# First stage of an RWKV and attention kernel: tile by tile, with two buffers for the mixes

## The reference, cut to what matters

```python
mod_x = jax.nn.silu(c) @ mod_w[i] + mod_b[i]        # and mod_c from c_ctx
sh_x, sc_x, g_x = jnp.split(mod_x[:, None, :], 3, axis=-1)
h_x = rmsnorm(x, norm_g[i]) * (1.0 + sc_x) + sh_x   # and h_c
prev = jnp.pad(h[:, :-1], ((0, 0), (1, 0), (0, 0)))
nxt = jnp.pad(h[:, 1:], ((0, 0), (0, 1), (0, 0)))
xx = 0.5 * (prev + nxt) - h
lerp = lambda j: h + xx * mu[j]
r, k, v, gate = (lerp(j) @ w_in[j] for j in range(4))   # 1024 x 1024 each
lerp(4) @ w1, lerp(5) @ a1                               # 128 columns each (two directions)
...
x = x + g_x * d_x                                    # d_x is the mixer's output
```

## Time and profile before

| | us |
|---|---|
| median of 3 runs | 4448.01 |
| lowest and highest | 4444.34 and 4450.34 |
| the profiled execution | 4446.85 |
| its span in the trace | 4445.1 |
| busy in it: PE, PEld, DVE, ACT, POOL | 3809.0, 2148.3, 1544.3, 1354.1, 206.0 |
| first stage, first product to last | 87.86 to 490.99 |
| mean granted clock of PE | 0.939 |

### The profile page before, as it was taken

One profiled execution on the slowest core, in us unless ns is written; L12 is line 12 of the kernel. 1 busy time (PEld: TensorE's weight loads), 2 busy tenths in 40 slices (PEclk: granted clock), 3 DMA queues, 4 the chain that ended last, 5 costly groups with the idle time before them and its releaser, 6 DMA issues. The chain is left out here.

```text
span 4445.1 us, 76078 instructions
## 1 busy us (share of the span) xinstructions
PE 3809.0 (86%) x32246; PEld 2148.3 (48%) x32246; DVE 1544.3 (35%) x3747; ACT 1354.1 (30%) x2940; POOL 206.0 (5%) x199
## 2 busy tenths in 40 slices
PE   5999577777787699999898888999959988699997
PEld 2555366666666444666466543333335455233332
DVE  2000366666676112443236531111122174211112
ACT  2000234444433122332446422222224263222221
POOL 0000000000000000010010000000012000000000
PEclk7999789989999899999999989999979999899998
DMA  5221434334444220000210049999933010899996
GB/s 206 74 92 49 130 96 120 101 106 118 121 111 114 85 106 1 20 1 23 77 59 1 1 155 334 386 395 392 399 138 94 11 39 1 293 388 393 389 391 269
DMA packets 315052, 697.62 MB, mean 157 GB/s; under 512 B 169168, under 2 KB 195920, under 8 KB 289616
## 3 DMA queue, kind: packets, MB, share of 16 engines
q1 hardware_dynamic: 293488, 613.98, 38.7%
q0 software_dynamic: 14048, 53.49, 3.4%
q10 hardware_dynamic: 7168, 25.17, 1.4%
HBM read 625.72 MB, written 64.50 MB: 155 GB/s over the span
## 5 line engine op out<-in xcount | busy, mean ns | idle before, releaser
L200 PE MATMUL ps<-arena 128*128 128x384 f32 (+8 forms) x5516 | 1599.9, 454 | 186.9 <-issue 38.7
L200 PEld LDWEIGHTS ps<-arena 128*128 128x128 f32 (+4 forms) x5516 | 917.2, 193 | 837.3 <-issue 460.6
L2635 PE MATMUL ps<-arena 128*32 128x512 f32 x9216 | 1025.7, 598 | 30.8 <-DMA arena<-in_w 26.2
L2635 PEld LDWEIGHTS ps<-arena 128*32 128x32 f32 x9216 | 305.0, 110 | 653.5 <-issue 636.5
L576 PE MATMUL ps<-arena 64*64 64x64 f32 (+1 forms) x10624 | 459.9, 240 | 179.6 <-DVE arena L1137 64.5
L576 PEld LDWEIGHTS ps<-arena 64*64 64x64 f32 x10624 | 411.0, 145 | 258.9 <-issue 101.0
L2769 DVE COPY arena<-ps 128x384 f32<-128x384 f32 x64 | 35.7, 557 | 671.0 <-PE ps L2694 671.0
L206 PE MATMUL ps<-arena 128*128 128x128 f32 x1200 | 191.7, 295 | 80.4 <-DVE arena L3083 40.7
L2745 ACT ACTIVATE arena<-ps 96x512 f32<-96x512 f32 x64 | 38.0, 593 | 625.7 <-PE ps L2635 625.7
L206 PEld LDWEIGHTS ps<-arena 128*128 128x128 f32 x1200 | 145.3, 154 | 122.2 <-DVE arena L3083 44.2
L549 DVE SCALAR_TENSOR_TENSOR arena<-arena 128x768 f32<-128x768 f32 x48 | 45.1, 1013 | 353.0 <-PE ps L200 353.0
(11 more groups left out here) (281 smaller groups left out, 3614.5 us busy)
## 6 DMA issues: line engine op xcount, KB each, us to landing
arena<-in_w SPq DMA_DIRECT2D x192, 2048.0 KB, 30.1
arena<-in_w_mod SPq DMA_DIRECT2D x24, 2048.0 KB, 9.0
arena<-in_mod_w SPq DMA_DIRECT2D x12, 2048.0 KB, 15.9
yb<-arena ACTq DMA_DIRECT2D x64, 384.0 KB, 9.9
arena<-in_rwkv_w_in SPq DMA_DIRECT2D x8, 2048.0 KB, 10.9
rkvg<-arena POOLq DMA_DIRECT2D x32, 384.0 KB, 2.6
arena<-rkvg SPq DMA_DIRECT2D x32, 384.0 KB, 3.8
arena<-di SPq DMA_DIRECT2D x192, 64.0 KB, 2.6
```

The costliest lines, as they stand in the source:

```text
L200: ins = pe.matmul(out, l, r, start=(i == 0), stop=(i == len(pairs) - 1))
L2635: return pe.matmul(bank[32 * at:32 * at + 32, :], left[:, k, 32 * g:32 * g + 32], right[:, k, :], start=first, stop=last)
```

## The change

- The modulation of the first stage is cut to four pieces, in the order 2, 3, 0, 1 (scale, then shift). The pieces 4 and 5 (the gate) move to the scan, where they are the first of now 32; the scan uses the beats 280 and 284 too. What waited for 30 waits for 32.
- H, XX and the mixes are 772 columns wide, with a zero column before x, between x and ctx, and behind ctx (`pad`), so that one addition over 769 columns makes the neighbour sums of both streams. Mixed tokens of x start at column 1, those of ctx at 514 (`mixed`).
- DVE goes tile by tile: scale tile k + 1, then for tile k the addition, the half less H, and the first mix. Each waits for its forerunner. POOL's part of the shift and the wide instructions are gone.
- The first piece of product weights is multiplied by channel tile: for each k the eight groups' matmuls, into the eight banks, as soon as the mix of tile k is there.
- The groups of products are x (512 columns) and ctx (256) in place of two halves of 384.
- There are two buffers for mixes: mix j waits until the products of mix j - 2 are done.
- The squares go to the first mix buffer, and the four stages lie elsewhere in the arena.

```diff
--- before.py
+++ after.py
-            for v, a, n in self.streams:
-                dve.scalar_tensor_tensor(self.H[:, k, a:a + n], self.K.X[:, k, a:a + n], self.GS[:, k, v:v + 1], self.rstd[:, a:a + n],
-                                         ALU.mult, ALU.mult).then_inc(self.scaled, 1)
+            self.dve_tile(dve, k)
+
+    def tokens(self, k, v, a, n):
+        a += self.pad * (v + 1)
+        return self.H[:, k, a:a + n]
+
+    def dve_tile(self, dve, k):
+        for v, a, n in self.streams:
+            dve.scalar_tensor_tensor(self.tokens(k, v, a, n), self.K.X[:, k, a:a + n], self.GS[:, k, v:v + 1], self.rstd[:, a:a + n],
+                                     ALU.mult, ALU.mult).then_inc(self.scaled, 1)
...
-                act.activation(self.H[:, k, a:a + n], self.H[:, k, a:a + n], ACT.Identity, bias=self.MOD[:, self.sh + k, v:v + 1]
+                act.activation(self.tokens(k, v, a, n), self.tokens(k, v, a, n), ACT.Identity, bias=self.MOD[:, self.sh + k, v:v + 1]
...
-        self.H = K.take(KT, T)
-        xl = K.top
-        self.XX, self.LP = K.take(KT, T), K.take(KT, T)
-        XL = K.arena[:, xl:xl + 3 * SLOT]
-        self.modslots = self.slots + [XL[:, i * SLOT:(i + 1) * SLOT] for i in range(3)]
+        self.stage = [K.take(T) for _ in range(4)]
+
+        self.H = K.take(KT, self.W)
+        xx = K.top
+        self.XX, self.LPs = K.take(KT, self.W), [K.take(KT, self.W) for _ in range(2)]
+        self.modslots = self.slots + [K.arena[:, xx:xx + SLOT]]
         self.rstd, self.GS = K.take(T), K.take(KT, 2)
         self.modq = [K.take(512) for _ in range(2)]
-        self.stage = [K.take(T) for _ in range(4)]
-        self.sums = Sums(K, "in", [self.H[:, k, :] for k in range(KT)], self.rstd, T)
-        self.norm = Norm(K, "in", self.H, self.rstd, self.GS, K.PR("norm_g0"), K.MODS[0], 0, 8, self.sums)
-        self.modland = [K.land(i) for i in range(6)]
+        self.sums = Sums(K, "in", [self.LPs[0][:, k, 0:T] for k in range(KT)], self.rstd, T)
+        self.norm = Norm(K, "in", self.H, self.rstd, self.GS, K.PR("norm_g0"), K.MODS[0], 0, 8, self.sums, pad=1)
+        self.modland = [K.land(i) for i in range(4)]
         self.chunks = [(K.I["rwkv_w_in"][j], c * 512, 512) for j in range(4) for c in range(2)]
         self.chunks += [(K.I["rwkv_w1"], 0, 128), (K.I["rwkv_a1"], 0, 128)]
         self.land = [K.land(c % 3) for c in range(10)]
 
         self.used = [8 * (c + 1) for c in range(8)] + [66, 68]
...
+    W = T + 4
+    MODS = (2, 3, 0, 1)
...
-        for c in range(6):
-            sp.dma_start(kview(self.modslots[c], KT, 512), kchunk(K.I["mod_w"][0], c * 512, 512)).then_inc(self.modland[c][0], 16)
+        for i, c in enumerate(self.MODS):
+            sp.dma_start(kview(self.modslots[i], KT, 512), kchunk(K.I["mod_w"][0], c * 512, 512)).then_inc(self.modland[i][0], 16)
...
-        for c in range(7):
-            if c < 6:
+        for c in range(5):
+            if c < 4:
...
-        pe.wait_ge(s["in_mod"], 6)
-        e = 0
-        for c, (_, _, n) in enumerate(self.chunks):
+        pe.wait_ge(s["in_mod"], 4)
+
+        w = kview(self.slots[0], KT, 512)
+        pe.wait_ge(*self.land[0])
+        for k in range(KT):
+            pe.wait_ge(s["in_lerp"], k + 1)
+            for e in range(8):
+                ins = pe.matmul(self.product(e), w[:, k, e // 2 * 128:e // 2 * 128 + 128], self.mixed(0, e % 2)[:, k, :], start=(k == 0),
+                                stop=(k == KT - 1))
+                if k == KT - 1:
+                    ins.then_inc(s["in_mm"], 1)
+        e = 8
+        for c in range(1, 10):
+            n = self.chunks[c][2]
             w = kview(self.slots[c % 3], KT, n)
             pe.wait_ge(*self.land[c])
+            i = c // 2 if c < 8 else c - 4
             if c % 2 == 0 or c == 9:
-                pe.wait_ge(s["in_lerp"], 8 * ((c // 2 if c < 8 else c - 4) + 1))
+                pe.wait_ge(s["in_lerp"], 8 * (i + 1))
             for j in range(n // 128):
-                for a, w_ in SEGS:
-                    if e >= 8:
-                        pe.wait_ge(s["in_evac"], e - 7)
-                    mm(pe, K.ps[:, e % 8, 0:w_], [(w[:, k, j * 128:(j + 1) * 128], self.LP[:, k, a:a + w_]) for k in range(KT)]
-                       ).then_inc(s["in_mm"], 1)
+                for v in range(2):
+                    pe.wait_ge(s["in_evac"], e - 7)
+                    x = self.mixed(i, v)
+                    mm(pe, self.product(e), [(w[:, k, j * 128:(j + 1) * 128], x[:, k, :]) for k in range(KT)]).then_inc(s["in_mm"], 1)
                     e += 1
...
+    STREAMS = ((0, TX), (TX, TC))
+
+    def mixed(self, i, v):
+
+        a, n = self.STREAMS[v]
+        return self.LPs[i % 2][:, :, a + 1 + v:a + 1 + v + n]
+
+    def product(self, e):
+        return self.K.ps[:, e % 8, 0:self.STREAMS[e % 2][1]]
...
-        for c in range(6):
+        for c in range(4):
...
-            for a, n in SEGS:
...
+            for a, n in self.STREAMS:
...
-                act.activation(self.stage[st][:, a:a + n], K.ps[:, e % 8, 0:n], ACT.Copy).then_inc(s["in_evac"], 1)
+                act.activation(self.stage[st][:, a:a + n], self.product(e), ACT.Copy).then_inc(s["in_evac"], 1)
...
-        for c in range(6):
-            dve.wait_ge(s["in_mod_cols"], c + 1)
-            dve.tensor_tensor(K.MODS[0][:, 4 * c:4 * c + 4, :], K.ps[:, 4 + (c + 1) % 2, 0:8].rearrange("p (j v) -> p j v", v=2),
+        H, norm = self.H, self.norm
+        for v, at in enumerate((0, 1 + TX, 2 + T)):
+            dve.memset(H[:, :, at:at + 1], 0.0).then_inc(s["in_pad"], 1)
+        for i, c in enumerate(self.MODS):
+            dve.wait_ge(s["in_mod_cols"], i + 1)
+            dve.tensor_tensor(K.MODS[0][:, 4 * c:4 * c + 4, :], K.ps[:, 4 + (i + 1) % 2, 0:8].rearrange("p (j v) -> p j v", v=2),
                               mod_bias(K, c, "mod_b0"), ALU.add).then_inc(s["in_mod"], 1)
-        dve.wait_ge(s["in_mod"], 6)
-        self.norm.dve_gains(dve)
-        self.norm.dve_scale(dve)
-        H, XX, LP = self.H, self.XX, self.LP
-        self.norm.wait_all(dve)
-        for a, n in ((0, TX), (TX, TC)):
-            dve.tensor_tensor(XX[:, 0:5, a + 1:a + n - 1], H[:, 0:5, a:a + n - 2], H[:, 0:5, a + 2:a + n], ALU.add
-                              ).then_inc(s["in_shift"], 1)
-        dve.wait_ge(s["in_shift"], 2)
-        dve.wait_ge(s["in_shift_pool"], 6)
-        dve.scalar_tensor_tensor(XX, XX, 0.5, H, ALU.mult, ALU.subtract).then_inc(s["in_shift"], 1)
-        dve.wait_ge(s["in_shift"], 3)
-        for j in range(6):
-            if j:
-                dve.wait_ge(s["in_mm"], self.used[2 * j - 1 if j < 5 else 8])
+        dve.wait_ge(s["in_mod"], 4)
+        norm.dve_gains(dve)
+        dve.wait_ge(norm.gain, 4)
+        dve.wait_ge(self.sums.rooted, 2)
+        dve.wait_ge(s["in_pad"], 3)
+        norm.dve_tile(dve, 0)
+        for k in range(KT):
+            if k < KT - 1:
+                norm.dve_tile(dve, k + 1)
+            self.dve_shift(dve, k)
+            self.dve_mix(dve, 0, k)
+        for j in range(1, 6):
+
+            if j >= 2:
+                dve.wait_ge(s["in_mm"], self.used[2 * j - 3])
             for k in range(KT):
-                dve.scalar_tensor_tensor(LP[:, k, :], XX[:, k, :], K.PR("mu")[:, 8 * j + k:8 * j + k + 1], H[:, k, :],
-                                         ALU.mult, ALU.add).then_inc(s["in_lerp"], 1)
+                self.dve_mix(dve, j, k)
+
+    def dve_shift(self, dve, k):
+
+        H, XX, shift, n = self.H[:, k, :], self.XX[:, k, :], self.s["in_shift"], self.W - 3
+        self.norm.wait_tile(dve, k)
+        dve.tensor_tensor(XX[:, 1:n + 1], H[:, 0:n], H[:, 2:n + 2], ALU.add).then_inc(shift, 1)
+        dve.wait_ge(shift, 2 * k + 1)
+        dve.scalar_tensor_tensor(XX[:, 1:n + 1], XX[:, 1:n + 1], 0.5, H[:, 1:n + 1], ALU.mult, ALU.subtract).then_inc(shift, 1)
+        dve.wait_ge(shift, 2 * k + 2)
+
+    def dve_mix(self, dve, j, k):
+        n = self.W - 3
+        dve.scalar_tensor_tensor(self.LPs[j % 2][:, k, 1:n + 1], self.XX[:, k, 1:n + 1], self.K.PR("mu")[:, 8 * j + k:8 * j + k + 1],
+                                 self.H[:, k, 1:n + 1], ALU.mult, ALU.add).then_inc(self.s["in_lerp"], 1)
...
-        H, XX = self.H, self.XX
-        self.norm.wait_all(pool)
-        for a, n in ((0, TX), (TX, TC)):
-            pool.tensor_tensor(XX[:, 5:8, a + 1:a + n - 1], H[:, 5:8, a:a + n - 2], H[:, 5:8, a + 2:a + n], ALU.add
-                               ).then_inc(s["in_shift_pool"], 1)
-            pool.tensor_copy(XX[:, :, a:a + 1], H[:, :, a + 1:a + 2]).then_inc(s["in_shift_pool"], 1)
-            pool.tensor_copy(XX[:, :, a + n - 1:a + n], H[:, :, a + n - 2:a + n - 1]).then_inc(s["in_shift_pool"], 1)
...
-        self.chunks = [(K.I["mod_w"][1], 1, c, K.MODS[1], "mod_b1", 0) for c in range(6)]
+        self.chunks = [(K.I["mod_w"][0], 0, c, K.MODS[0], "mod_b0", 0) for c in range(4, 6)]
```

(18 more changed lines are left out.)

## The result

The changed kernel takes 4369.65 us (median of 4 runs, 4367.48 to 4374.36) against 4446.18 us before: the ratio is 0.9819 (95% interval 0.9800 to 0.9838), 76.5 us less. A second set gave 4365.71 us against 4438.93, ratio 0.9835 (0.9821 to 0.9848), 73.2 us less. The forecast was 4371.5.

The account below looks back on a forecast made before the run. It took the first stage's plain alternation of PE and DVE, with PE standing still, as what to shorten: 4446.85 - 89.4 (stage) + 14 (two late scan pieces) = 4371.5 us, range 4355 to 4385.

Parts of the forecast that it names:

- The bound and the frame: First stage: PE and DVE plainly alternate, so everything that shortens the stage shortens the span one for one.
- Part 1 (start of the norm): First stage's modulation: four pieces instead of six let the norm start at 42.35 us instead of 55.52.
- Rival (b): First stage: first product weights land up to 10 us late, delaying the start by up to 6.6: 4378 us; chance 0.05.
- Part 2 (tiles): Norm, shift, mix tile by tile: 4.0 us of DVE per tile, first product at 47.7 us instead of 87.86.
- Part 3 (streams): First stage's products: streams of 512 and 256 columns instead of 384 and 384, costed at nothing.
- rival (e): All 34 pairs of product groups: moving operands 4 or 8 bytes off read slower, 3.5 us per 1%; chance 0.05.
- Part 4 (two buffers): Changes of mix: a second buffer removes five PE gaps of 7.66 us and the slow start after each.
- Rival (d): First stage: a wait in the way leaves the five gaps and slow starts, +49.2 us, 4421; chance 0.03.
- Rival (c): First product piece by channel: clock stays at the lower level through its first round, +38.3 us, 4410; chance 0.05.
- Part 5 (the two late pieces): Scan's end, beats 280 and 284: two added modulation pieces wait for weights, 11.7 to 18.9 us late, 14 taken.
- The scan up to piece 29: Scan before its two new pieces: pieces 0 to 29 stand at the same beats as before.
- The signs: First stage and scan: first product at 47 to 49 us; 3 to 5 us idle before each of the last two sums.

Follow-up runs that it names:

- by group: The changed kernel with its first piece of products worked group by group after all eight mixes, not by channel tile: 4393.76 us, ratio 0.9884.
- the second trace: The changed kernel run again with nothing altered, for a second trace: 4365.71 us.

## Why the prediction was right, point by point

**The bound and the frame.** Right. The stage was a chain of DVE, then PE, then DVE; each microsecond taken out of it arrived at the start of the scan (89.8 us in the loads of the scan, 89.4 counted).

**Part 1 (start of the norm).** 42.05 us, counted 42.35. The weights of the first product were no bound: PE's wait of 6.00 us ended with DVE. Rival (b) did not occur in any trace: with four pieces and the product by channel the first product started at 46.98 to 47.57 us. With six pieces again it started 13.8 us later.

**Part 2 (tiles).** First product at 47.32, counted 47.7; tile 3.98, counted 4.0; the addition 0.95, where I had taken 0.96 over the 1.36 of the wide row. Undone, the product by channel was worth 26.8 us in the trace. PE did not wait within the first eight tiles, and the granted clock from 55 to 88 us was 1.00. The tile-by-tile work of DVE was not undone by itself; its share rests on the rows.

**Part 3 (streams).** Right at nothing: the evacuations of two groups of 512 columns in sequence, 98.61 and 108.93 us, are 10.32 us apart, as two groups of 384 were the earlier trace rows.

```profile
98.61 0.60 ACT L550 ACTIVATE arena<-ps 128x512 f32<-128x512 f32 x1 [6.43 <-PE ps L200]
102.06 0.38 ACT L550 ACTIVATE arena<-ps 128x256 f32<-128x256 f32 x1 [2.86 <-PE ps L200]
108.93 0.60 ACT L550 ACTIVATE arena<-ps 128x512 f32<-128x512 f32 x1 [6.48 <-PE ps L200]
```

The moving operands begin one and two elements off in these groups, so rival (e), the one that would have made the kernel slower, is refuted by the same rows.

**Part 4 (two buffers).** Counted 49.2 us, which is the stage's 89.4 less the 40.2 of the earlier start; five gaps and five slow starts of 2.3 add up to 49.8, so the prediction's two counts differ by 0.6. Measured are 47.8 by undoing it and 51.0 by adding it alone to the kernel before (first loads of the scan at 440.59 against 491.58), of which 1.6 lie ahead of the first product. Rival (d) is out. Rival (c) gave +38.3 us: the first piece took 44.4 us, and 41.6 at a clock of 1.00 with PE kept busy before it, so nothing of it is seen here. That rule of the Trainium skill (TensorE: Matmul & The Clock Gate, "A second HAM failure mode: psum-queue depth-cycling") is told of a bf16 kernel in which PE idles briefly between its groups; PE had no such gaps here, and this trace does not bear it out for a product that only changes its bank. The prediction's own row against it was worked out a little low: with 0.43 and 0.3225 us per record (5.16 / 16 by columns) it is 31.0 and not 30.7 us, an excess of 2.8.

**Part 5 (the two late pieces).** The mechanism and the place were right: two waits for weights, of 2.8 and 4.0 us, ended by DMA. The step that was mis-sized is its sum: 14 us taken, out of 11.7 to 18.9. Piece 29 to the last store is 19.6 us longer in the first trace and 16.5 in the second (48.9 - 32.4). But the tail's clock is in this. Without late pieces this stretch took 32.4 to 32.5 us in three traces with the tail's groups at 1.53 us, and 35.9 in two (the second buffer alone, and PE kept busy) with groups at 2.90 (34.9 in the run without the gate, at 2.62 and 2.90). With late pieces it took 48.8 and 48.9 us with the fast tail (by group, and the second trace) and 52.1 in two with the slow one. Like against like, the two pieces cost 16.2 to 16.5 us, 2.2 to 2.5 more than taken, and the tail's half clock, which I had not counted, 3.1 to 3.5; it belongs to no edit.

Where the 2.2 to 2.5 us come from: I had leant to the low end "because the other transfers of the scan have ended there". That holds for piece 30, which started 8.10 us after the sums of piece 29 ended, and not for piece 31, which started 9.85 us after those of piece 30 (8.05 and 9.58 in the second trace). SyncE, too, works its program in order: it waits for the sums of piece 30, issues the load of piece 31, and only then the tail's load of the gate, 384 KB, which the kernel before had issued long ago, at 1435.46, ahead of its piece 29:

```profile
1358.77 0.40 SPq L869 DMA_DIRECT2D arena<-in_w_mod  x1
1359.21 0.58 SPq L814 DMA_DIRECT2D arena<-rkvg  x1
```

The two loads travel together in all four traces with late pieces, which may be why the second wait is the longer one; no run isolates it. And the sums took 2.77 and 3.64 us (3.55 and 3.64), not 1.92, so I should have taken the half clock for both.

**The scan up to piece 29** was counted as unchanged. In the first trace it took 5.7 us less, which made up for the 5.6 us missing in part 5. That was luck, not insight. Kernels with the places of the 30 pieces unchanged took 949.8 (before), 946.9, 950.9, 945.9, 944.7, 944.1, 941.5 and 938.2 us for the same beats, with and without the change. The scatter of single traces is as large as the difference, and what decides it was not settled; the sums that ran at the half clock in some periods of the trace before (3.34 to 3.44 us in place of 1.92) are a candidate that no run isolated.

**The signs.** In the first trace they came as named, but for the first of the two waits (2.79 us, where 3 to 5 were named). The scan's end came 14.0 us later after its start than before (996.2 against 982.2 us), inside the 10 to 20 named. In the second trace it came only 4.9 us later (987.1), which the prediction had called a sign of being wrong. It was a bad sign to choose: it takes in the whole scan, whose length differs by up to 12.7 us from trace to trace. Counted from piece 29, both traces show the cost.

**The sum.** 4371.5 against a median of 4369.65 and 4365.71. The gain in the stage is shown, by the trace and by undoing its main parts. That the total agrees to 2 us in one set and 6 in the other owes something to the scatter of what lies behind the stage.

## What to carry to other kernels

Work that is moved "behind" other work is paid at its new place. Before moving it, read which engine is last in those very beats: the same two pieces cost some 16 us at the end of the scan and next to nothing at the beats 15 and 51, and a table of the busy time by engine for three beats points to such places. Such a table of the rest of the loop was worth about as much as the edit under study (73 to 77 us): the same pieces at other beats gave 55 us in the kernel before and 81 to 85 us in the changed one. It is a pointer, not a proof: the beats behind the places 27 and 33, chosen by the same rule, became 1.5 and 1.3 us longer.

When a stage alternates between two engines, count both halves of the price of a gap: the gap, and the slow start behind it (7.67 + 2.0 us here).

## What the runs showed that I had not expected

- The time of this kernel depends on its data: with the first layer's gate at zero nearly the same program needed 4555 us and 3400 instructions more. An experiment that leaves work out upstream of the expert layers must be read from its trace.
- The half clock comes and goes at the end of the scan without any edit near it: the same two groups took 1.53 us in eight traces (before among them) and 2.26 to 2.90 in six, some 3 us of the time.
- A load of 2 MB that was asked for when nothing else was queued was used 8.05 to 8.11 us later (piece 30, four traces), where 2.1 MB at the 387 GB/s of the earlier trace rows are 5.4 us; with a load of 384 KB right behind it, 9.56 to 9.85 (piece 31). A loop that reuses one slot pays for this wherever two uses stand closer than that: at seven of the 30 places before, 0.8 to 2.3 us each.
